# Running a decoder step's second half in three token blocks, with expert rows gathered between the instructions of the projections

## The reference, cut to what matters

```python
h = rms_norm(x, n_mix_pre) * (1 + sc1) + sh1
bg, cg, hin, q, k, v, r, ga, gb, alow = split(h @ w_in)
branch_a = (bg * short_conv(cg * hin)) @ w_proj_a
branch_b = (rms_norm(gla(q, k, v, alow)) * silu(r)) @ w_proj_b
m = (sigmoid(ga) * branch_a + sigmoid(gb) * branch_b) @ w_out
x = x + g1 * rms_norm(m, n_mix_post)
h = rms_norm(x, n_ffn_pre) * (1 + sc2) + sh2
# PEER: 8 heads, top 16 of 128*128 experts by product keys
s = einsum(h @ wq, subkeys); sv, si = top_k(s, 16)        # twice 128 keys a head
top_v, top_i = top_k(sv[0] + sv[1], 16); expert = ids; gate = softmax(top_v)
act = gelu(einsum(u_tab[expert], h))                      # 128 rows of u a token
p = einsum(gate * act, v_tab[expert])                     # 128 rows of v a token
x = x + g2 * rms_norm(p, n_ffn_post)
```

## Time and profile before

| what | value |
|---|---|
| median of 3 runs | 4821.8 us (4818.18 to 4822.32) |
| profiled execution, its own time | 4813.56 us |
| its span, first to last instruction | 4811.8 us |
| mean granted clock | 0.766 |
| busy: TensorE, VectorE, GpSimd, ScalarE | 68%, 49%, 29%, 11% of the span |
| HBM read | 1259.27 MB |

### The profile page before, as it was taken

The page is one execution under the profiler, slowest core; times in us unless marked ns, Lnnn a source line. Parts: engine busy times, 40 slices in busy tenths (PEclk is TensorE's granted clock), DMA queues, the critical chain, the costliest instruction groups (busy, mean ns, idle before and its releaser), DMA issues. The chain is left out here.

```text
span 4811.8 us, 43674 instructions
## 1 busy us (share of the span) xinstructions
PE 3292.1 (68%) x15775; PEld 1751.6 (36%) x15775; DVE 2358.9 (49%) x5057; ACT 551.5 (11%) x999; POOL 1412.9 (29%) x1297
## 2 busy tenths in 40 slices
PE   8688996988984992566665665565665666655674
PEld 2577885988983990111111111111111111111111
DVE  0355335300314676655555555556546555556543
ACT  1222222011013111000000000000000000000001
POOL 0311100222311111343433333433333434333330
PEclk9899998999997995666666666666666766666687
DMA  6110111022321104999999999999999999999996
GB/s 247 48 46 27 46 38 55 26 95 111 124 87 77 54 22 183 396 392 410 409 388 409 393 405 408 385 422 401 388 421 405 391 406 411 390 406 411 417 422 251
DMA packets 206836, 1302.03 MB, mean 271 GB/s; under 512 B 25537, under 2 KB 42561, under 8 KB 61266
## 3 DMA queue, kind: packets, MB, share of 16 engines
q0 software_dynamic: 156672, 1140.92, 57.5%
q1 hardware_dynamic: 47554, 140.09, 8.0%
q10 hardware_dynamic: 2448, 18.88, 1.0%
HBM read 1259.27 MB, written 40.54 MB: 270 GB/s over the span
## 5 line engine op out<-in xcount | busy, mean ns | idle before, releaser
L1632 DVE CUSTOM_DVE_ANT_0 peer_uv<-peer_uv,all_PS 128x1024 f32<-128x1024 f32 x1088 | 1313.1, 1220 | 1245.7 <-PE all_PS L1402 694.7
L1361 POOL DMA_INDIRECT peer_uv<-in_uv,peer_idx x1088 | 1052.6, 967 | 1778.9 <-PE all_PS L1416 1493.0
L1416 PE MATMUL all_PS<-peer_uv,peer_zw 128*32 128x512 f32 x4352 | 947.8, 982 | 583.7 <-DVE peer_zw L1611 579.2
L1402 PE MATMUL all_PS<-peer_hT,peer_sel 96*128 96x512 bf16 x2176 | 770.2, 467 | 441.5 <-DVE peer_dots L1632 439.7
L1402 PEld LDWEIGHTS all_PS<-peer_hT,peer_sel 96*128 96x128 bf16 x2176 | 167.3, 107 | 1245.5 <-DVE peer_dots L1632 759.8
L1416 PEld LDWEIGHTS all_PS<-peer_uv,peer_zw 128*32 128x32 f32 x4352 | 165.3, 152 | 1136.2 <-DVE peer_zw L1611 762.8
L1529 ACT ACTIVATE peer_ge<-peer_dots 128x4 f32<-128x4 f32 x272 | 56.1, 206 | 2631.6 <-DVE peer_dots L1632 2626.7
L124 PE MATMUL all_PS<-stream_h_hi,keys_w_hi 128*128 128x384 f32 (+1 forms) x384 | 127.2, 331 | 60.3 <-DVE keys_w_lo L1239 51.4
L133 POOL CAST gla_w_hi<-gla_w 128x1024 fp32r<-128x1024 f32 x24 | 27.7, 1153 | 426.6 <-DMA gla_w<-in_w_heads 273.5
L124 PE MATMUL all_PS<-stream_h_hi,side_w_hi 128*128 128x384 f32 (+1 forms) x384 | 126.4, 329 | 16.8 <-DVE side_w_lo L771 16.8
L124 PE MATMUL all_PS<-stream_h_hi,gla_w_hi 128*128 128x384 f32 (+1 forms) x384 | 126.0, 328 | 1.8 <-DVE gla_low L641 1.8
(11 more groups left out here) (293 smaller groups left out, 4960.7 us busy)
## 6 DMA issues: line engine op xcount, KB each, us to landing
cond_w<-in_w_ada SPq DMA_DIRECT2D x12, 2048.0 KB, 7.7
peer_uv<-in_uv,peer_idx POOLq DMA_INDIRECT x1088
gla_w<-in_w_heads SPq DMA_DIRECT2D x24, 512.0 KB, 3.3
scratch_sig<-side_sig ACTq DMA_DIRECT2D x8, 1088.0 KB, 4.0
merge_sig<-scratch_sig ACTq DMA_DIRECT2D x8, 1088.0 KB, 5.0
side_w<-in_w_gate_ab SPq DMA_DIRECT2D x16, 512.0 KB, 3.2
keys_w<-in_w_query SPq DMA_DIRECT2D x16, 512.0 KB, 3.2
conv_w<-in_w_conv SPq DMA_DIRECT2D x12, 512.0 KB, 3.2
```

The lines of the kernel that those rows point to most:

```text
L1361: nc.gpsimd.indirect_dma_start(out=uv[:, n % NUV, :], out_offset=None, in_=A["uv"], in_offset=bass.IndirectOffsetOnAxis(ap=idx[:, t % 2, r ...
L1402: last = nc.tensor.matmul(PS[:, 2 * (n % 2) + e, :], sel[:, c, :], hT[:, t % 2, j, e * 512:(e + 1) * 512], start=True, stop=True)
L1416: last = nc.tensor.matmul(PS[j * GR:(j + 1) * GR, 4 + e, :], zw[:, z, GR - 1 - c:2 * GR - 1 - c], uv[:, n % NUV, D + e * 512:D + (e + 1) * ...
L1632: nc.vector.tensor_tensor_reduce(u, u, PS[:, 2 * (n % 2):2 * (n % 2) + 2, :].rearrange("p b d -> p (b d)"), 1.0, 0.0, ALU.mult, ALU.add, d ...
```

## The change

`condition_phase` and `heads_phase` stay (the first also writes h and four modulation rows to HBM). Everything from the convolution to the picking of experts is run three times, for blocks of 320, 384 and 384 tokens (`BLOCKS`, three tiles each in the order 0, 1, 8, 2 to 7). In a block there are six phases, each still a `Scope` with a barrier at its end: `mix` (conv and gate, 28 steps), `merge` (16), `out` (12), `norm` (9), `keys` (18), `pick` (13). A step is one weight block's product for the block's tokens (24 matmuls of 320 or 384 columns; in `out` the operands are swapped: 24 matmuls of 256 columns; in `norm` and `pick` a piece of the work of a tile). So each weight block is loaded and split three times instead of once. The high part is made by ScalarE after the step's product, the low part by GpSimd. Inputs of a phase (`Halves`) come from HBM chunk by chunk and are split by ScalarE and VectorE.

`Gather` keeps its buffers through all phases. Behind each step every engine runs its part of the gather for a share of the tokens of the block before: 24 tokens in the first block's `pick`, 296 in the second block (76, 39, 33, 32, 59, 57 in its six phases), 384 in the third (99, 50, 43, 42, 77, 73). The last 384 tokens are done in `drain_phase` with nothing beside them. GpSimd fetches four tokens further than the share (`AHEAD`). There are 10 row buffers instead of 11; each half of a token's h goes to one bank and is used by an own VectorE instruction of 512 elements, with no second pair of banks (the four banks from `FRONT` on belong to the block's products); a small VectorE sum joins the halves for each four tokens. The h pieces are made in `norm` and go through HBM; the last norm and residual are done per tile, token by channel, and `final_phase` is gone. All of the picking is done in `pick`, before the block's tokens may be gathered.

```diff
+BLOCKS = ((0, 3), (3, 6), (6, 9))
+class Gather:
+    NUV, NZ, ND, NH, AHEAD = 10, 3, 4, 6, 4
+    def fetch(self, pool, upto):
+        for n in self.steps("pool", upto + self.AHEAD if upto else 0):
+            if n == self.before[u]:
+                pool.wait_ge(self.M["idx_set"], u + 1)
+            if n >= self.NUV:
+                pool.wait_ge(self.M["v_mm"], (n - self.NUV) // BT + 1)
+            nc.gpsimd.indirect_dma_start(out=self.uv[:, n % self.NUV, :], ...)
+    def spread(self, pe, upto):
+        for n in self.steps("pe", upto):
+            for f in range(2):
+                if n:
+                    pe.wait_ge(M["dotted"], 2 * (n - 1) + f + 1)
+                nc.tensor.matmul(PS[:, f, :], self.sel[:, c:c + 1].broadcast_to([3 * GR, P]),
+                                 self.hT[:, g % self.NH, f * 512:(f + 1) * 512], ...).then_inc(M["h_spread"], 1)
+            if n % BT == 1 and n >= BT:
+                self.summed(pe, n // BT - 1)
+    def dots(self, dve, upto):
+        for n in self.steps("dve", upto):
+            dve.wait_ge(self.uv_in[s], 16 * (n // self.NUV) + 16)
+            for f in range(2):
+                dve.wait_ge(M["h_spread"], 2 * n + f + 1)
+                nc.vector.tensor_tensor_reduce(part, part, PS[:, f, :], 1.0, 0.0, ALU.mult, ALU.add,
+                                               self.halves[:, d, f, e:e + 1]).then_inc(M["dotted"], 1)
+                if f == 0 and e == 0 and q:
+                    self.weigh(dve, q - 1)
+            if e == BT - 1:
+                nc.vector.tensor_tensor(self.pre[:, d, :], self.halves[:, d, 0, :], self.halves[:, d, 1, :], ...)
+def mix_phase(nc, A, G, part, gat, lo, hi):
+        upto = lambda j: share(lo, hi, j, NJ)
+        def _(pool):
+            for j in range(NJ):
+                w.make_low(nc, pool, j + w.pairs)
+                gat.fetch(pool, upto(j))
+        def _(pe):
+            for j in range(NJ):
+                pe.wait_ge(...)                      # bank of step j - 4 read
+                w.product(nc, pe, j, bank(j), h)
+                gat.spread(pe, upto(j))
+        def _(act):
+            for j in range(NJ):
+                act.wait_ge(w.used, j + 1)
+                nc.scalar.activation(...)            # bank(j) read
+                w.make_high(nc, act, j + w.pairs)
+                gat.gelu(act, upto(j))
+        def _(dve):
+            for j in range(NJ):
+                ...
+                gat.dots(dve, upto(j))
-            conv_phase(nc, A, G)
-            gate_phase(nc, A, G)
-                merge_phase(nc, A, G)
-                out_phase(nc, A, G)
-                keys_phase(nc, A, G)
-        gather_phase(nc, A, G)
-        final_phase(nc, A, G)
+            WEIGHTS = (26, 13, 11, 11, 20, 19)
+            for part in parts:
+                mix_phase(nc, A, G, part, gat, marks[0], marks[1])
+                merge_phase(nc, A, G, part, gat, marks[1], marks[2])
+                    out_phase(nc, A, G, part, gat, m_rows, marks[2], marks[3])
+                    norm_phase(nc, A, G, part, gat, m_rows, marks[3], marks[4])
+                    keys_phase(nc, A, G, part, gat, best, place, marks[4], marks[5])
+                    pick_phase(nc, A, G, part, gat, best, place, marks[5], marks[6])
+            drain_phase(nc, gat)
```

More of the change, by code:

```diff
@@ L730, in _ @@
                 assert step.n == OWN
[L733 to L790, removed]
@@ new lines, with __init__ @@
+BLOCKS = ((0, 3), (3, 6), (6, 9))
+BT = 4
+FRONT = 4
+class Part:
+    def __init__(self, index, first, last):
+        self.index, self.tiles = index, range(first, last)
+        self.rows = [rows(ORDER[u]) for u in self.tiles]
+        self.at = [sum(self.rows[:i]) for i in range(len(self.rows))]
+        self.n = sum(self.rows)
+        self.samples = NT - 1 in ORDER[first:last]
+        self.prompt = self.n - TAIL * self.samples
+        self.spans = []
+        for i, u in enumerate(self.tiles):
+            start = ORDER[u] * P
+            if self.spans and sum(self.spans[-1][1:]) == start:
+                self.spans[-1] = self.spans[-1][:2] + (self.spans[-1][2] + self.rows[i],)
+            else:
+                self.spans.append((self.at[i], start, self.rows[i]))
@@ L993, in merge_phase, with out_phase @@
+def out_phase(nc, A, G, part, gat, m_rows, lo, hi):
+    with Scope(nc, f"out{part.index}") as sc:
+        n, PS = part.n, G["PS"]
+        nt, WC = len(part.tiles), 256
+        x = Halves(sc, "x", KD, n, [(0, 0, n)], lambda k, at, m: A["merged"][:, k, part.index, 0:n])
+        w = Stream(sc, [A["w_out"][q] for q in range(D // WC)], cols=WC, raws=1, pairs=2, per=nt)
+        m_out = sc.sem("m_out")
         block = sc.block()
-        sets = lambda n: [PS[:, 3 * n + b] for b in range(3)]
+        NJ = w.count * nt
+        bank = lambda j: PS[0:part.rows[j % nt], FRONT + j % 4, 0:WC]
+        upto = lambda j: share(lo, hi, j, NJ)
@@ L1039 @@
[L1039 to L1064 removed]
+            for k in range(KD):
+                x.make_low(nc, dve, k)
@@ new lines, in _, with norm_phase @@
+            for j in range(NJ):
+                gat.dots(dve, upto(j))
+def norm_phase(nc, A, G, part, gat, m_rows, lo, hi):
+    with Scope(nc, f"norm{part.index}") as sc:
+        PS, nt = G["PS"], len(part.tiles)
+        R = part.rows
+        x = sc.sb("x", [P, nt, D])
+        gb = sc.sb("gb", [P, 3, D])
+        gs = sc.sb("gs", [TAIL, 3, D]) if part.samples else None
+        tmp = sc.sb("tmp", [P, 2, D])
+        ss, root = sc.sb("ss", [P, 2, nt]), sc.sb("root", [P, 2, nt])
+        first, third, fourth = (sc.sb(q, [P, D], BF16) for q in ("first", "third", "fourth"))
+        second = sc.sb("second", [P, D])
+        hT = sc.sb("hT", [P, 2, KD, P])
+        gb_in, squared, logged, rooted, own, x2_done, h2_done = (sc.sem(q) for q in (
+            "gb_in squared logged rooted own x2_done h2_done").split())
+        x_in = [sc.sem(f"x_in{i}") for i in range(nt)]
+        one, two, three, four, x2_saved, p_saved, t_mm, t_out, t_saved = (sc.sem(q) for q in (
+            "one two three four x2_saved p_saved t_mm t_out t_saved").split())
@@ new lines, in _ @@
+        @block.tensor
+        def _(pe):
+            for j in range(NJ):
+                i, q = divmod(j, PARTS)
+                if q == 0 and i:
+                    pe.wait_ge(own, OPS * i)
+                    if i >= 2:
+                        pe.wait_ge(r_out, 2 * (i - 1))
+                    for e in range(3):
+                        last = nc.tensor.transpose(PS[:, FRONT, e * P:(e + 1) * P], route[:, e, :], G["ident"][:, :])
+                    last.then_inc(r_mm, 1)
+                gat.spread(pe, upto(j))
```

1528 lines of the change are left out of this document (826 added, 702 removed).

## The result

The changed kernel takes 5071.3 us (median of 4 runs, 5064.2 to 5078.9) where the kernel before takes 4820.0 in the same session: ratio 1.0528, 95% interval 1.0499 to 1.0557. The profiled execution has a span of 5077.0 us, 265 above that of before. I had forecast 5000 (span 4996) and 73% for slower.

What follows compares the result with a forecast made beforehand. It took the gather as bound by DMA and the 1019 us before it by TensorE with some VectorE. Summed: 820 + 10 + 590 + 2 * (510 + 155) + 1224 + 1010 + 12 = 4996, forecast 5000 us, range 4680 to 5230.

Steps and rivals of the forecast that it cites:

- the ledger: Whole kernel: savings of 564 and 56 us against +610 for two blocks, +182 first block, 10 writing; together +182.
- Token in a step: 1.8 us: Gather token inside a block's step: dots 1.4 plus exposed v sum 0.4 us; bounds 1.4 and 2.15.
- Sum 510: Block of 384 tokens without its gather tokens: mix 153, merge 70, out 36, norm 40, keys 103, pick 108 us.
- starts and ends 155: Starts and ends of a block's six phases: 155 us a block, bounds 100 and 280.
- 45 were booked: Ends of a block's phases: 45 us for the writes that the barriers wait for.
- the products at 5.3 us: TensorE's product of 24 matmuls of 384 columns in a step: 5.3 us at a mean granted clock of 0.8.
- 4 us behind its product, four tokens ahead ... also under 11.8: GpSimd's late fetches in a mix step are covered: DMA work at most 10.5 us, under a step of 11.8.
- Tokens cost only the dots: Rival, steps in blocks: v sums run during VectorE's own block work, a token costs 1.4 us; 4724 us, 25%.
- The clock falls back: Rival, TensorE in blocks: products at the lower clock take 7.7 us, tokens 2.15; 5540 us, half of it 5270; 8%.
- No overlap to speak of: Rival, steps in blocks: DMA idles in each product and tokens keep 2.63 us; 5560 us, 5%.
- Loads beside the gather: Rival, phase starts: each of 12 waits for the four fetched tokens, 10.5 us more each; 5122 us, 12%.

Runs made afterwards that it cites:

- the interleaving: Changed kernel with the tokens' spreads and sums between the product's chunks and each engine's gather part ahead of its own work: 4929.6 us, ratio 1.0224.
- fetches first: Changed kernel with only GpSimd's order changed, a step's fetches ahead of the low part of the next weights: 5019.9 us, ratio 1.0418.
- the run without a share: Changed kernel with no tokens gathered inside the three blocks, all 1088 in the drain: 5350.2 us, ratio 1.1094.
- block 2's half share: Changed kernel with the shares of blocks 2 and 3 halved to 148 and 266 tokens, 650 in the drain: 5023.6 us, ratio 1.0419.
- the kernel with interleaved projections and pick: Kernel with tokens placed between the product's chunks, plus VectorE's dots between the instructions of a pick part: 4871.8 us, ratio 1.0110.
- Tokens in the starts: Kernel with interleaved projections and pick, plus 66 tokens gathered in the starts of mix, merge, out and keys of blocks 2 and 3: 4865.2 us, ratio 1.0095.

## Why the prediction was right, and where its terms were off

**Direction and mechanism held.** The kernel is slower because three blocks cost more than the overlap gives: I had +182 in the ledger, the spans say +265. That a token in a step still pays for TensorE and VectorE taking turns is borne out by the interleaving: same instructions, same shares, and it took 142 us off, of which GpSimd's order alone gave 51 in a run of its own.

**Two terms were off, against each other,** and that the sum of 4996 lies only 81 below the span is in part luck: 283 too low, 210 too high, block 1 another 17 too low, what stands ahead of it 9 too high. (a) *Token in a step: 1.8 us* was too low; it measured 2.22 over both blocks ((649 + 858) / 680), above my upper bound of 2.15. That is 283 us. (b) *Sum 510* and *starts and ends 155* were too high: an empty later block is 560, which is 105 less twice. Of that 105, some 33 are the writes at phase ends: 45 were booked, and in the empty block 2 the six phases end 1 to 4 us after their last own instruction, 12 us in all. Another 40 are the products at 5.3 us: without tokens mix runs at a granted clock of 0.94 and a product takes 4.3 us there and 4.5 in keys ((5.3 - 4.3) * 28 + (5.3 - 4.5) * 16 = 41). The rest is spread over the steps and starts. With tokens the clock of mix falls to 0.84 and 0.81 and a product takes 4.9 us, so even there 5.3 was too much; those 0.6 us come with the tokens and belong to their price.

**What the 1.8 left out.** It added a dot chain and a share of the sum, and took the DMA engines as covered: "4 us behind its product, four tokens ahead ... also under 11.8". In block 2 the cover held; there fetches first changed mix by nothing. In block 3, with 3.5 tokens a step, it did not: in the step shown VectorE's dots follow the landings at 2.5 us, and fetches first took 25 us off that mix phase (381 to 355). It also left out the ends of phases: with tokens, block 2's phases end 12 to 21 us after their last own instruction, where the empty ones end after 1 to 4. There the last step's tokens run with no product beside them. That the price rises with the tokens in a step (1.57, then 2.82) the prediction had not considered at all, and it is the finding that matters most: the mean of 2.2 looks like a gain over 2.63, and the last token put in is a loss.

**Point by point.** Block 1: 607 for 590, first gather at 1322.95 us for 1320. Blocks 2 and 3: 1207 and 1419 for 1198 and 1356. Drain and tail 1023 for 1022, DMA share 0.98. DMA share in the blocks 0.80 and 0.84, at and above the 0.6 to 0.8 named. Dots 684 ns for 0.6 to 0.7 us. Mix steps 11.1 and 13.6 us for 10 to 12, so block 3's are outside. TensorE's idle time up to the end of a phase's first product is 11 to 12 us in mix and keys, 18 in out and 6 in merge, where 20 to 30 was named. Clock 0.78 and 0.75 for 0.8. VectorE was 76 and 79% busy in pick, not over 80%, and yet on the path.

**The rivals.** *Tokens cost only the dots* (1.4): refuted as a mean by the run without a share; only the 148 tokens of block 2's half share come near (1.57). *The clock falls back*: true in small part. Some products start at the lower level (the one shown at 0.58), but only 12 of 54 take over 5.5 us, and the mean is 4.9 us, below my 5.3 and far from 7.7. The Trainium skill (TensorE: Matmul & The Clock Gate, HAM oscillation) has bursts separated by waits start throttled; this trace agrees for the first 3.8 us of the product shown, 0.58, and not for the one at 2911.68 us, which comes right behind a sum of v rows of 3.35 us and ran at 1.00. *No overlap to speak of* (2.63): wrong as a mean (2.22); the tokens added last cost even more than that (2.82 and 2.76). *Loads beside the gather* (10.5 us more for each start): no run moved the loads apart from the gathers, but the traces speak against it. Measured from a phase's first load, the first whole product of blocks 2 and 3 ends after 19.4 and 21.1 us in mix, 25.6 and 24.8 in out, 20.6 and 20.4 in keys, 11.0 and 11.0 in merge. In the kernel without a share it ends after 18.9 and 19.5, 24.0 and 24.2, 22.3 and 22.5, 11.2 and 12.0.

**What stays open.** In the kernel with interleaved projections and pick the DMA engines still idle for 0.15 * 1126 + 0.09 * 1295 = 286 us of blocks 2 and 3. Tokens in the starts took 5 to 13 us off out of both blocks and merge of block 2 and 9 off its keys, but mix of block 2 rose by 9 and keys of block 3 by 23, from 262 to 286 us: why these rose is not settled. The ends of the phases, where the last step's tokens run alone, were not attacked, and neither was the picking, which makes half of the 539 us. Two pairs of banks for h inside the blocks were not tried.

## What to carry to other kernels

Before work is split into blocks so that two stages overlap, measure the split without any overlap: here it cost 539 us, and the overlap gave 273 back. Look in it for work that was hidden before and now lies on the path: here picking was half of it. Price overlapped work at its margin and not by its mean, with a run at half the share; where the margin is above the price outside, put less in. And "overlapped" in the program's order is not overlapped on the engines: the same instructions placed between a product's chunks, with the fetches ahead of the weight splitting, were worth 142 us.

## What the runs showed of the hardware that was not expected

- With a DMA share of 0.84 over block 3, the engines ran at 1.0 for a stretch inside it (2835.6 to 2849.6 us) and idled elsewhere; removing 51.4 MB of their work from both blocks, 128 us at 402 GB/s, gave 24 to 40 us.
- The granted clock moved within a single step of 14 us: 0.58 in the product's first 3.8 us, 0.94 to 1.0 in the next 5.2, 0.69 in the spreads. Another product of the same phase ran at 1.00 from start to end.
- A pair of spreads took 0.61 us at a clock of 1.00 (2841.59) and 1.22 in the stretch at 0.69 (2846.42), with VectorE's dots unchanged at 0.69 us. Not all of that is the clock: a single spread takes 0.39 and 0.61 us, and the second of the later pair had to wait for a dot.
